# Two stacked blocks on one core: bias tables and a third gate unit earlier in the state-space loop, first units by input quarters, GpSimd's sum behind the level loop

## The chip, the cores and the metric

The kernel runs on one NeuronCore of a Trainium2 chip. Its time is the device time of one launch in microseconds (us), the median of three runs. TensorE (PE) multiplies, VectorE (DVE), ScalarE (ACT) and GpSimd (POOL) do the elementwise work, SyncE (SP) starts the loads of the weights. Every engine takes its own instructions in order; between engines there are only semaphores.

## The reference, cut to what matters

256 tokens of width 1024 pass through two blocks. All numbers are float32.

```python
# first block, two layers
h = rms_norm(x) * (1 + sc1) + sh1
x = x + gt1 * hybrid_mixer(h)           # w_in, gated delta rule, stick-breaking attention, w_out
h = rms_norm(x) * (1 + sc2) + sh2
x = x + gt2 * (swiglu(h) if l == 0 else moe_swiglu(h))   # d_ff 3584; top 2 of 8 experts
# second block, two layers
h = h + 0.5 * swiglu(rmsnorm(h))        # ffn1, d_ff 2816
u = rmsnorm(h)
h = h + (s5_mixer(u) if layer == 0 else nsa_mixer(u, kv))
h = h + 0.5 * swiglu(rmsnorm(h))        # ffn2
```

In the delta rule each of 16 chains (8 heads, 2 chunks) needs `decay = exp(g_i - g_j)` for the triangle that is kept, once for the matrix that is inverted and once, transposed, for `qk = (q k^T) * decay`. The S5 mixer is a complex diagonal recurrence over 256 steps for 64 groups of 64 states, then a GELU, then `y * sigmoid(y @ w_glu)`. The attention of the last layer adds a bias by the distance between query and key, one number per head out of a small table `rel_bias`; for the compressed keys these are 15 columns for each of 16 heads and two tiles of tokens.

## The kernel before, in words

**Weights.** All large weights lie in DRAM as units of 128 x 2048 numbers (1 MB). SP loads them into a ring of six buffers in the order of use; a buffer is loaded again when TensorE has reported the unit before in it as done (`unit_done`). For most units ScalarE writes a rounded high part (`w_hi`, line 2484, into one of two places), VectorE the rest (`w_low`, line 1384, as are all its plain two-input operations), and TensorE sums three products: high by high, high by low part of the input, low part by high (`product`, lines 523 to 525). A unit has 16 tiles, so 48 matmuls of 256 columns. Some units (the gate units of S5, w_kv, w_q, w_o) are multiplied in plain float32 instead, at two PE instructions a matmul (lines 464 and 1099).

**The first unit of a stage.** The input is split as well, in four quarters of two 128-row tiles: ScalarE writes the high part of quarter c (semaphore `h_high`, lines 2567 and 2525), VectorE the low part (`h_low`, lines 1384 and 1415). `cols_split` goes over the two output tiles t and, within t, over the eight input tiles k, with all three products of a tile together; for t = 0 it waits for `h_low` of a quarter before the quarter's first product, and t = 1 needs no wait any more. `cols_raw` is the form for the stages whose input isn't scaled by its norm yet (`ffn2_0`, `ffn2_1`): both t over k = 0 to 5, then both t over k = 6, 7, with the same waits. Behind it stands the sum of the squares for the norm (line 474). Seven stages begin in one of these ways: `w_in0`, `ffn`, `w_in1`, `ffn1_0`, `ffn2_0`, `ffn1_1`, `ffn2_1`.

**The S5 loop.** For each of eight rounds k: TensorE multiplies the input (`pair_inputs`, line 1134, banks 0 to 3), VectorE rotates the sums, scans twice (lines 2239, 2240) and rotates back; TensorE forms the outputs of the round (`pair_outputs`, lines 1149 to 1157, bank 4), ScalarE the GELU (`s5_gelu`, line 2856). TensorE's order by hand is: outputs of round k-1, inputs of round k+1, for k < 5 the transposes of matrices (line 480, into bank 5, copied out by ScalarE, semaphore `bt`), for k = 5, 6, 7 ten small products each of the bias table (`bias_tables`, line 1111, 32 rows by 16 columns, also into bank 5), and one row of the gate product for units 0 and 1 (`glu_row`, line 1099, banks 6 and 7). Units 2 and 3 of the gate go to banks 0 and 1, which are free once VectorE has read the last inputs; their rows 0 to 3 stand at k = 7, the rest after the last outputs. ScalarE's round is: GELU of round k-2, the row of magnitudes for the scan (line 2871), the copies of bank 5 for k < 5, a diagonal (line 2882). After the loop VectorE turns bank 5 into the bias table, ScalarE takes four sigmoids (line 2889), VectorE updates x and `ffn2_0` begins.

**The delta mixer.** The 16 triangular matrices are inverted in six levels (`squares`, line 610, and VectorE, lines 1384, 1883, 1891); `level_f` counts VectorE's updates of the inverse, ten in all. Beside it GpSimd makes the second decay: clamp (line 2999), add of a mask kept in `inverse_rms` (line 3001, reports `u_arg`), later two products (3003, 3005, reports `q_decayed`). ScalarE's order is: copies of qk (2752), two silus, wait for `u_arg`, exp (2756), two sigmoids of the gates (2758), then the copies that TensorE's `corner(1)` waits for (`neg_b`, line 2760) and those for `corner_b` (2762). TensorE's order there is: turn(2, 0) (line 653), corner(0), corner(1) (line 610), three more turns, z(0), z(1), the products for v_new (line 701).

Of the kernel before, what the change touches and what calls it, by code (L numbers as in the profile page):

```python
# [22 lines left out]
P = 128  # L23
# [68 lines left out]
def program(nc, A):  # L92
    ctx = ExitStack()
    with ctx:
# [5 lines left out]
        def sem(name):  # L100
            if name not in sems:
# [5 lines left out]
                         attn_tensor=("bias_ps", "hid_ps", "hid_t_ps", "cmp_ps", "kv_sum", "kv_vt", "kc_sum", "gate_logits",  # L107
                                      "cmp_logits"),
                         attn_scalar=("hid", "kv_rs", "kc_rs", "gate_exp", "cmp_exp"))
# [170 lines left out]
        GLU_BANK = (6, 7, 0, 1)  # L280
# [166 lines left out]
        def _(pe):  # L447
# [79 lines left out]
            def cols_raw(n, dst, room, name):  # L527

                for k0, k1 in ((0, 6), (6, KT)):
                    for t in range(2):  # L530
                        for k in range(k0, k1):
                            if t == 0 and k % 2 == 0:
                                pe.wait_ge(*at("h_low", k // 2 + 1, INPUTS[name]))
                            c = (k * 2 + t) * P
                            mm = product(dst(t), parts(w_high(room, n) + c, P), ring_low[n % RING][:, c:c + P],
                                         parts(h_high(room) + k * TOK, TOK), parts(HB + k * TOK, TOK), k == 0 and t == 0,
                                         k == KT - 1, skip_group_check=True)
                mm.then_inc(sem("unit_done"), 1)

            def cols_split(n, dst, room, first=None, low=HB):  # L540

                for t in range(2):
# [413 lines left out]
            def ffn_split(name, blocks, base, room):  # L956
# [3 lines left out]
                def step(p, i=0):  # L960
# [8 lines left out]
                    if which < 2:  # L969
# [3 lines left out]
                        if p == 0 and name in UNSCALED:  # L973
                            cols_raw(n, lambda t: half(0, t), room, name)
# [116 lines left out]
            def glu_row(k, first):  # L1091

                pe.wait_ge(sem("y_gelu"), k + 1)
                for u in (first, first + 1):
# [9 lines left out]
            def bias_tables(part):  # L1104

                if part == 0:
                    pe.wait_ge(sem("bt"), 6)
                for j in range(10 * part, 10 * part + 10):
                    n, c = divmod(j, NCMP)
                    x = 255 + n * P - 16 * c - 31  # L1110
                    mm = pe.matmul(bank[5][:, j * QH:(j + 1) * QH], con("onehot", P, x, pn=32),
                                   par("rel_bias", 16, pn=32), start=True, stop=True)

# [59 lines left out]
            pair_inputs(1)  # L1173
            for k in range(1, KT + 1):
# [8 lines left out]
                if k > 4 and k < KT:  # L1183
                    bias_tables(k - 5)
                if k > 1:
                    glu_row(k - 2, 0)
                if k == KT - 1:

                    pe.wait_ge(sem("bu_read"), KT)
                    for r in range(4):  # L1190
                        glu_row(r, 2)
            for r in range(4, KT - 1):
                glu_row(r, 2)
            glu_row(KT - 1, 0)
            glu_row(KT - 1, 2)
# [183 lines left out]
        def _(ve):  # L1379
# [872 lines left out]
            ve.wait_ge(*event("bias_ps"))  # L2252
            for n in range(NT):

                tt(view(BIG, CB + n * QH * NCMP, [[NCMP, QH], [1, NCMP]]), view(bank[5], n * QH * NCMP, [[1, QH], [QH, NCMP]]),
# [218 lines left out]
        def _(se):  # L2474
# [391 lines left out]
            for k in range(KT):  # L2866
# [15 lines left out]
                act(big(D_DIAG + k % 4 * P, P), ident, ACT.Copy, scale=par("s5_d", 1, k)).then_inc(sem("s5_scalar"), 1)  # L2882
            s5_gelu(KT - 2)
# [91 lines left out]
        def _(po):  # L2975
# [18 lines left out]
            for l in range(LAYERS):  # L2994
# [5 lines left out]
                b16 = view(BIG, SLOT["B"], [[P, 16], [1, P]])  # L3000
                po.tensor_tensor(b16, b16, view(RS, 0, [[0, 16], [1, P]]), ALU.add).then_inc(mixer("u_arg", l)[0], 1)
# [215 lines left out]
```

## Time and profile before

| | |
|---|---|
| median of three runs | 3108.93 us (3107.57 to 3109.07) |
| the profiled execution: its own time, its span | 3107.27 us, 3105.5 us |
| busy: PE, DVE, ACT, POOL | 97%, 73%, 52%, 2% |
| mean granted TensorE clock | 0.977 of 2.4 GHz |
| HBM read | 698.5 MB, 225 GB/s over the span |

The span runs from the first to the last instruction. In rows of the timeline the first number is the start in us from the start of the span, the second the duration; `xN` is how many instructions a row merges, and `[idle before <-releaser]` how long the engine had nothing to do before it and what ended that.

### The profile page before, as it was taken

How to read it: one execution, taken by the hardware profiler on the slowest of the kernel's cores; microseconds unless marked ns; L12 is line 12 of the kernel's file. 1: busy time of each engine (PE TensorE's matmuls, PEld its weight loads, DVE VectorE, ACT ScalarE, POOL GpSimd, SP SyncE). 2: the span in 40 equal slices, each digit the busy share in tenths (PEclk: the TensorE clock that was granted, in tenths of full speed). 3: DMA queues.
4: the chain of work that ended last, by engine and by line, in shares of the span. 5: the costliest groups of instructions: out<-in, count | busy, mean ns of one | idle time of the engine just before them, and what ended most of it. 6: DMA issues, size and time to landing. Idle time of an engine off the chain costs nothing.

```text
span 3105.5 us, 51419 instructions
## 1 busy us (share of the span) xinstructions
PE 3013.7 (97%) x21686; PEld 2740.2 (88%) x21686; DVE 2268.9 (73%) x2596; ACT 1624.5 (52%) x1604; POOL 74.2 (2%) x83
## 2 busy tenths in 40 slices
PE   7999999999999999999999999999899999998999
PEld 7998899999988788888888888899779999996899
DVE  7977688848685888888888888688665536547355
ACT  3444543435553777777777777543324414436333
POOL 0002000000010000000000000000000000000000
PEclk8999999989999999999999999999899999999999
DMA  8650488735403799999999999745234544540353
GB/s 358 253 190 2 159 312 314 259 113 183 150 2 136 256 365 370 366 366 367 371 364 365 370 366 367 268 164 187 97 123 176 181 158 150 202 163 28 125 187 122
DMA packets 130030, 703.14 MB, mean 226 GB/s; under 512 B 11184, under 2 KB 15552, under 8 KB 74048
## 3 DMA queue, kind: packets, MB, share of 16 engines
q1 hardware_dynamic: 118816, 650.30, 57.1%
q0 software_dynamic: 6880, 48.24, 4.0%
q8 instruction: 128, 2.10, 0.3%
q10 hardware_dynamic: 4160, 2.12, 0.3%
q14 instruction: 46, 0.38, 0.0%
HBM read 698.50 MB, written 1.07 MB: 225 GB/s over the span
## 4 chain that ended last, share of the span: by engine, by line
PE 91%; DVE 6%; ACT 2%; issue 1%; DMA 0%; SPq 0%; ACTq 0%; DVEq 0%
PE banks L523 25%; PE banks L524 25%; PE banks L525 25%; PE banks L464 3%; PE banks L474 1%; DVE ring_low L1384 1%; DVE tail L1384 1%; PE banks L610 1%; PE banks L1099 1%; DVE big L1384 1%; PE banks L851 1%; PE banks L519 1%; PE banks L872 1%; ACT parts L2484 0%; PE banks L1157 0%
## 5 line engine op out<-in xcount | busy, mean ns | idle before, releaser
L1384 DVE TENSOR_TENSOR ring_low<-ring,parts 128x2048 fp32r<-128x2048 f32 x586 | 1333.2, 2288 | 365.2 <-ACT parts L2484 339.6
L523 PE MATMUL banks<-parts 128*128 128x256 f32 (+1 forms) x3968 | 1240.1, 313 | 15.1 <-DVE tail_parts L1384 7.0
L524 PE MATMUL banks<-tail_parts,parts 128*128 128x256 f32 x3744 | 1060.5, 283 | 0.0
L2484 ACT ACTIVATE parts<-ring 128x2048 fp32r<-128x2048 f32 x250 | 479.1, 1917 | 776.3 <-PE banks L525 730.4
L525 PE MATMUL banks<-parts,ring_low 128*128 128x256 f32 x3072 | 868.7, 283 | 0.0
L523 PEld LDWEIGHTS banks<-parts 128*128 128x128 f32 x3968 | 753.7, 190 | 57.3 <-issue 12.4
L2586 ACT ACTIVATE parts<-ring 128x2048 fp32r<-128x2048 f32 x336 | 644.5, 1919 | 188.5 <-DMA ring<-in_wall 181.3
L524 PEld LDWEIGHTS banks<-tail_parts,parts 128*128 128x128 f32 x3744 | 710.9, 190 | 2.0 <-issue 1.9
L525 PEld LDWEIGHTS banks<-parts,ring_low 128*128 128x128 f32 x3072 | 584.5, 190 | 0.0
L525 PE MATMUL banks<-parts,tail_parts 128*128 128x512 f32 x896 | 352.6, 393 | 0.0
L524 PE MATMUL banks<-ring_low,parts 128*128 128x512 f32 x896 | 352.5, 393 | 0.0
L523 PE MATMUL banks<-tail_parts,parts 128*128 128x256 f32 x928 | 262.7, 283 | 0.1
L525 PE MATMUL banks<-tail_parts,ring_low 128*128 128x256 f32 x928 | 262.2, 283 | 0.0
L525 PEld LDWEIGHTS banks<-parts,tail_parts 128*128 128x128 f32 x896 | 168.3, 188 | 40.5
L524 PEld LDWEIGHTS banks<-ring_low,parts 128*128 128x128 f32 x896 | 168.8, 188 | 33.9
L523 PE MATMUL banks<-parts,tail_parts 128*128 128x512 f32 x448 | 177.5, 396 | 1.1 <-DVE tail_parts L1384 1.0
L523 PEld LDWEIGHTS banks<-tail_parts,parts 128*128 128x128 f32 x928 | 176.7, 190 | 0.4 <-issue 0.4
L525 PEld LDWEIGHTS banks<-tail_parts,ring_low 128*128 128x128 f32 x928 | 176.4, 190 | 0.0
L524 PE MATMUL banks<-ring_low,tail_parts 128*128 128x512 f32 x448 | 176.3, 394 | 0.0
L525 PE MATMUL banks<-parts 128*128 128x512 f32 x448 | 176.2, 393 | 0.0
L1384 DVE TENSOR_TENSOR tail_parts<-banks,tail_parts 128x256 fp32r<-128x256 f32 x112 | 47.4, 424 | 85.8 <-ACT tail_parts L2612 85.5
L1384 DVE TENSOR_TENSOR tail<-tail,banks 128x256 f32<-128x256 f32 (+1 forms) x164 | 81.7, 498 | 31.0 <-PE banks L525 19.4
(451 smaller groups left out, 3155.0 us busy)
## 6 DMA issues: line engine op xcount, KB each, us to landing
ring<-in_wall SPq DMA_DIRECT2D x616, 1024.0 KB, 6.1
big<-in_wall POOLq DMA_DIRECT2D x40, 1024.0 KB, 5.8
big<-in_w_k POOLq DMA_DIRECT2D x1, 2048.0 KB, 8.1
big<-in_w_v POOLq DMA_DIRECT2D x1, 2048.0 KB, 13.7
big<-bias_table ACTq DMA_DIRECT2D x2, 1024.0 KB, 7.2
constants<-in_con SPq DMA_DIRECT2D x1, 1249.5 KB, 9.3
x<-in_x SPq DMA_DIRECT2D x1, 1024.0 KB, 6.6
big<-big POOLq DMA_DIRECT2D x16, 64.0 KB, 5.1
```

The lines of the kernel that those rows point to most:

```text
L464: mm = pe.matmul(dst(t), tile(n, k * tiles + t), src[:, src_off + k * width:src_off + (k + 1) * width], start=(k == 0), stop=(k == kt - 1))
L474: mm = pe.matmul(half(b, 0), ones, big(SQ0 + t * TOK, TOK), start=(t == 0), stop=(t == KT - 1))
L519: mm = pe.matmul(o[:, c:c + 1], ada_sum(first + n)[:, t * P:(t + 1) * P], ones[:, 0:1], start=True, stop=True)
L523: pe.matmul(o, high, in_high, start=start, stop=False, **kw)
L524: pe.matmul(o, high, in_low, start=False, stop=False, **kw)
L525: return pe.matmul(o, low, in_high, start=False, stop=stop, **kw)
L610: mm = pe.matmul(bank[b][SQ * h:SQ * h + SQ, c % 8 * SQ:(c % 8 + 1) * SQ], lhs(c, h), rhs(c, h), start=True, stop=True)
L851: mm = pe.transpose(bank[6 + b % 2][:, f * P:(f + 1) * P], FG[:, b % 2 * 512 + f * P:b % 2 * 512 + (f + 1) * P], ident)
L872: mm = pe.matmul(bank[k][:, :], parts(source + n * 1024 + k * P, P), parts(SEL + n * 1024 + batch * 512, 512), start=(part == 0 and n == 0 ...
L1384: return ve.tensor_tensor(out, a, b, op)
L2484: act(parts(w_high(room, n), UNIT), ring[n % RING][:, :], ACT.Copy).then_inc(sem("w_high"), 1)
L2586: act(parts(slot_at(q), UNIT), ring[r][:, :], ACT.Copy).then_inc(sem("x_high"), 1)
```

## The change

It has three parts. None changes what is computed.

**1. The S5 loop.** The thirty bias products are made in two halves of fifteen, the first behind the inputs of round 1, the second at k = 1 behind the transposes, into bank 7. ScalarE copies them at k = 1 to `LNB` and `RS` (two new copies of 128 x 240), after a wait for the new event `bias_rows` and ahead of its GELU of round 0; TensorE waits for `bias_raw` at k = 2, before the gate product writes bank 7. Unit 2 of the gate moves to bank 5 and joins at k = 5, with its rows 0 to 2 first; unit 3 moves to bank 0.

**2. First units.** `cols_chunks` takes the place of `cols_raw` and of `cols_split` for a stage's first unit, where the low part lies at `HB`: for each quarter it waits for `h_high`, makes the eight products that need only the high part, waits for `h_low` and makes the other four.

**3. The delta mixer.** GpSimd's add waits for the tenth `level_f`.

```diff
-        GLU_BANK = (6, 7, 0, 1)
+        GLU_BANK = (6, 7, 5, 0)
...
+            def cols_chunks(n, dst, room, name):
+
+                for c in range(4):
+                    pe.wait_ge(*at("h_high", c + 1, INPUTS[name]))
                     for t in range(2):
-                        for k in range(k0, k1):
...
+                        for k in (2 * c, 2 * c + 1):
+                            w = (k * 2 + t) * P
+                            high = parts(h_high(room) + k * TOK, TOK)
+                            pe.matmul(dst(t), parts(w_high(room, n) + w, P), high, start=(k == 0 and t == 0), stop=False,
+                                      skip_group_check=True)
+                            pe.matmul(dst(t), ring_low[n % RING][:, w:w + P], high, start=False, stop=False, skip_group_check=True)
+                    pe.wait_ge(*at("h_low", c + 1, INPUTS[name]))
+                    for t in range(2):
+                        for k in (2 * c, 2 * c + 1):
+                            mm = pe.matmul(dst(t), parts(w_high(room, n) + (k * 2 + t) * P, P), parts(HB + k * TOK, TOK), start=False,
+                                           stop=(k == KT - 1), skip_group_check=True)
                 mm.then_inc(sem("unit_done"), 1)
 
             def cols_split(n, dst, room, first=None, low=HB):
 
+                if first is not None and low == HB:
+                    cols_chunks(n, dst, room, first)
+                    return
...
             pair_inputs(1)
+            bias_table(0)
             for k in range(1, KT + 1):
                 pair_outputs(k - 1)
...
                     turn_matrices(k + 3, bank[5]).then_inc(sem("bt_ps"), 1)
-                if k > 4 and k < KT:
-                    bias_tables(k - 5)
+                if k == 1:
+                    bias_table(1).then_inc(event("bias_rows")[0], 1)
+                if k == 2:
+                    pe.wait_ge(*event("bias_raw"))
+                if k == 5:
+                    pe.wait_ge(sem("bt"), 6)
+                    for r in range(k - 2):
+                        glu_row(r, (2,))
                 if k > 1:
-                    glu_row(k - 2, 0)
+                    glu_row(k - 2, (0, 1) if k < 5 else (0, 1, 2))
                 if k == KT - 1:
 
                     pe.wait_ge(sem("bu_read"), KT)
                     for r in range(4):
-                        glu_row(r, 2)
+                        glu_row(r, (3,))
             for r in range(4, KT - 1):
-                glu_row(r, 2)
-            glu_row(KT - 1, 0)
-            glu_row(KT - 1, 2)
+                glu_row(r, (3,))
+            glu_row(KT - 1, (0, 1, 2, 3))
...
                 act(big(D_DIAG + k % 4 * P, P), ident, ACT.Copy, scale=par("s5_d", 1, k)).then_inc(sem("s5_scalar"), 1)
+                if k == 1:
+                    se.wait_ge(*at("normed", KT, 6))
+                    se.wait_ge(*event("bias_rows"))
+                    act(LNB[:, 0:QH * NCMP], bank[7][:, 0:QH * NCMP], ACT.Copy)
+                    act(RS[:, 0:QH * NCMP], bank[7][:, QH * NCMP:2 * QH * NCMP], ACT.Copy).then_inc(event("bias_raw")[0], 1)
...
                 b16 = view(BIG, SLOT["B"], [[P, 16], [1, P]])
+                po.wait_ge(*at("level_f", 2, l, 2 * LEVELS - 2))
                 po.tensor_tensor(b16, b16, view(RS, 0, [[0, 16], [1, P]]), ALU.add).then_inc(mixer("u_arg", l)[0], 1)
```

## Rows read from the trace of the kernel before

**Rows 1.** The page, its chain that ended last, by engine.

```profile
PE 91%; DVE 6%; ACT 2%; issue 1%; DMA 0%; SPq 0%; ACTq 0%; DVEq 0%
```

**Rows 2.** Timeline of DVE in the S5 loop: start, us, engine, operation, idle before.

```profile
2219.26 1.22 DVE L1384 TENSOR_TENSOR big<-banks,big 128x1024 f32<-128x1024 f32 x1
...
2240.87 1.22 DVE L2239 TENSOR_TENSOR_SCAN big<-small,big 128x512 f32<-128x512 f32 x1 [1.20 <-ACT small L2871]
...
2245.59 1.22 DVE L1384 TENSOR_TENSOR tail<-big 128x1024 f32<-128x1024 f32 x1 [1.12 <-PE banks L1157]
...
2287.86 1.22 DVE L1384 TENSOR_TENSOR tail<-big 128x1024 f32<-128x1024 f32 x1
```

**Rows 3.** Timeline of PE at the loop's head, outputs of rounds 0 and 1.

```profile
2227.76 1.22 PE L1149 MATMUL banks<-tail,big 128*128 128x256 f32 x2 [4.59 <-DVE tail L1384]
...
2240.34 1.19 PE L1149 MATMUL banks<-tail,big 128*128 128x256 f32 x2 [3.85 <-ACT big L2856]
```

**Rows 4.** Timeline of PE at the loop's end.

```profile
2285.51 2.40 PE L1111 MATMUL banks<-parameters,constants 32*128 32x16 f32 x20
2287.84 8.90 PE L1099 MATMUL banks<-big,ring 128*128 128x256 f32 x40
...
2299.96 10.63 PE L1099 MATMUL banks<-big,ring 128*128 128x256 f32 x48
```

**Rows 5.** Timelines of DVE, ACT and PE at the start of ffn2_0.

```profile
2317.49 0.88 DVE L1415 SCALAR_TENSOR_TENSOR tail_parts<-x,parameters,parts 128x256 fp32r<-128x256 f32 x2 [0.25 <-ACT parts L2525]
...
2320.50 2.19 ACT L2531 ACTIVATE tail<-x 128x512 f32<-128x512 f32 x4
...
2323.56 3.62 PE L474 MATMUL banks<-tail,constants 128*128 128x256 f32 x16
```

**Rows 6.** Timeline of PE in the first units of ffn, ffn1_0 and ffn1_1.

```profile
386.51 0.55 PE L523 MATMUL banks<-parts 128*128 128x256 f32 x1 [3.95 <-DVE tail_parts L1384]
...
390.81 0.39 PE L523 MATMUL banks<-parts 128*128 128x256 f32 x1 [0.37 <-DVE tail_parts L1384]
...
2021.23 0.39 PE L523 MATMUL banks<-parts 128*128 128x256 f32 x1 [0.41 <-DVE tail_parts L1384]
...
2577.10 0.36 PE L523 MATMUL banks<-parts 128*128 128x256 f32 x1 [1.88 <-DVE tail_parts L1384]
```

**Rows 7.** Timelines of POOL and DVE in the delta mixers of layers 0 and 1.

```profile
245.15 4.52 POOL L3001 TENSOR_TENSOR big<-big,inverse_rms 128x2048 f32<-128x2048 f32 x1
...
246.55 3.67 DVE L1384 TENSOR_TENSOR tail<-constants,big 128x512 f32<-128x512 f32 x1
251.58 0.69 DVE L1384 TENSOR_TENSOR tail<-constants,big 128x512 f32<-128x512 f32 x1
...
271.15 0.65 DVE L1384 TENSOR_TENSOR tail<-tail,banks 128x512 f32<-128x512 f32 x1
...
853.57 4.56 DVE L1384 TENSOR_TENSOR tail<-constants,big 128x512 f32<-128x512 f32 x1
```

**Rows 8.** Windows: us, busy PE, PEld, DVE, ACT, POOL, granted clock, DMA, GB/s.

```profile
252.00:256.00 4.00, 3.92 (x74) 3.74 (x72) 2.25 (x4) 3.97 (x3) 2.43 (x1) 0.50 0.01 4
...
2328.00:2332.00 4.00, 4.00 (x36) 4.00 (x35) 2.02 (x1) 3.23 (x3) 0.00 (x0) 1.00 0.02 4
```

**Rows 9.** Timeline of ACT in the first mixer, from the exp on.

```profile
251.59 1.91 ACT L2756 ACTIVATE big<-big 128x2048 f32<-128x2048 f32 x1
253.51 1.28 ACT L2758 ACT_TABLE_LOAD   x1
254.81 3.71 ACT L2758 ACTIVATE big<-big 128x2048 f32<-128x2048 f32 x2
278.84 0.59 ACT L2760 ACTIVATE tail<-banks 64x512 f32<-64x512 f32 x1 [20.32 <-PE banks L638]
```

**Rows 10.** Timeline of PE in the first mixer, both corners, three turns.

```profile
279.76 2.08 PE L610 MATMUL banks<-tail,big 64*64 64x64 f32 x32
281.76 2.84 PE L653 MATMUL banks<-constants,big 128*128 128x128 f32 x24
```

More of the change, by code:

```diff
@@ L106, in program @@
                                       "k_normed", "cmp_arg", "cmp_p"),
-                         attn_tensor=("bias_ps", "hid_ps", "hid_t_ps", "cmp_ps", "kv_sum", "kv_vt", "kc_sum", "gate_logits",
+                         attn_tensor=("bias_rows", "bias_ps", "hid_ps", "hid_t_ps", "cmp_ps", "kv_sum", "kv_vt", "kc_sum", "gate_logits",
                                       "cmp_logits"),
-                         attn_scalar=("hid", "kv_rs", "kc_rs", "gate_exp", "cmp_exp"))
+                         attn_scalar=("bias_raw", "hid", "kv_rs", "kc_rs", "gate_exp", "cmp_exp"))
         def event(name):
@@ L525, in product @@
                 return pe.matmul(o, low, in_high, start=False, stop=stop, **kw)
-            def cols_raw(n, dst, room, name):
-                for k0, k1 in ((0, 6), (6, KT)):
+            def cols_chunks(n, dst, room, name):
+                for c in range(4):
+                    pe.wait_ge(*at("h_high", c + 1, INPUTS[name]))
                     for t in range(2):
-                        for k in range(k0, k1):
[L532 to L537, printed above, removed]
+                        for k in (2 * c, 2 * c + 1):
[9 more added lines that the diff above has]
+                                           stop=(k == KT - 1), skip_group_check=True)
                 mm.then_inc(sem("unit_done"), 1)
             def cols_split(n, dst, room, first=None, low=HB):
+                if first is not None and low == HB:
+                    cols_chunks(n, dst, room, first)
+                    return
                 for t in range(2):
@@ L973, in step @@
                         if p == 0 and name in UNSCALED:
-                            cols_raw(n, lambda t: half(0, t), room, name)
+                            cols_chunks(n, lambda t: half(0, t), room, name)
                             norm(7 if name == "ffn2_0" else 11, NORM_BANK[7 if name == "ffn2_0" else 11], RAW_SQ)
@@ L1089, in _, with glu_row @@
             pe.wait_ge(sem("bt"), 1)
-            def glu_row(k, first):
+            def glu_row(k, units):
                 pe.wait_ge(sem("y_gelu"), k + 1)
-                for u in (first, first + 1):
+                for u in units:
                     n = UN["glu"] + u
@@ L1102, in glu_row, with bias_table @@
                         mm.then_inc(sem("unit_done"), 1)
[L1104 to L1109, printed above, removed]
+            def bias_table(n):
+                for c in range(NCMP):
                     x = 255 + n * P - 16 * c - 31
-                    mm = pe.matmul(bank[5][:, j * QH:(j + 1) * QH], con("onehot", P, x, pn=32),
+                    j = n * NCMP + c
+                    mm = pe.matmul(bank[7][:, j * QH:(j + 1) * QH], con("onehot", P, x, pn=32),
                                    par("rel_bias", 16, pn=32), start=True, stop=True)
+                return mm
             def distance_table():
@@ L2252, in _ @@
             ve.wait_ge(*event("bias_ps"))
+            ve.wait_ge(*event("bias_raw"))
             for n in range(NT):
-                tt(view(BIG, CB + n * QH * NCMP, [[NCMP, QH], [1, NCMP]]), view(bank[5], n * QH * NCMP, [[1, QH], [QH, NCMP]]),
+                tt(view(BIG, CB + n * QH * NCMP, [[NCMP, QH], [1, NCMP]]), view((LNB, RS)[n], 0, [[1, QH], [QH, NCMP]]),
                    view(CON, CC["cmp_add"] + n * NCMP, [[0, QH], [1, NCMP]]), ALU.add)
```

## The prediction

> **What bounds the kernel now.** I read the page's chain first: 91% of the chain that ended last is TensorE [rows 1]. In the long stages its products follow one another without a gap, and nothing in this change touches them. So I went on to the waits, looking for the stretches where TensorE waits or runs at half its clock, and then to the timelines of the three places that the change edits. The reader is to see three things. In the S5 loop VectorE works nearly without a break from 2219.26 to 2289.1 us [rows 2], and TensorE waits for it in the first rounds [rows 3] but is behind it in the last: the outputs of the last round could start at 2289.1, and start after 2296.7, where a backlog of gate products ends [rows 4]. In the first unit of a stage TensorE waits for VectorE's low parts [rows 6]. In the delta mixer one VectorE addition that takes 0.69 us alone takes 3.67 and 4.56 us [rows 7]. Everything else between is rigid: a microsecond won in one of these places should arrive at the end, since the loads follow TensorE's reports through a ring of six.
>
> The sum is made against the profiled execution's own time, 3107.27 us; the median of the runs shown is 3108.93, that is 1.7 more, and I carry the difference over unchanged.
>
> **Part 1, the S5 loop: the end of it.** A PE instruction of the gate product costs 8.90 / 40 = 0.22 us, a table product (two instructions) 2.40 / 10 = 0.24 [rows 4]. From 2285.5 on TensorE has today: ten table products 2.3, 40 gate instructions 8.9, the distance table and the outputs together about 3.3 (2296.7 to 2300.0), 48 gate instructions 10.6, end 2310.6 [rows 4]. After the change the rounds 5 and 6 hold 24 and 12 gate instructions in place of 20 table and 8 gate instructions each: 5.3 and 2.6 us for 4.0 and 4.0. So round 5 is a microsecond longer, inside a wait for VectorE, and round 6 ends before VectorE has its result, so the outputs of round 6 start about 1.2 us earlier than today and run into no backlog. Then: outputs 2280.7 to 2283.4, 12 + 16 gate instructions 6.1 us to 2289.5, just at VectorE's 2289.1; distance table and outputs 3.3 to 2292.8; 12 + 12 + 16 = 40 instructions 8.8 us to 2301.5. That is 9.1 us before today's 2310.6. What is late next is nothing: the GELU of the last round and the split of the first `ffn2_0` unit move with the outputs and stay ahead of the last row.
>
> **Part 1, the head of it.** The first fifteen table products fall into a gap of 4.59 us [rows 3]. At full clock they cost 15 x 0.24 = 3.6 us and are hidden; at half clock, which this gap has, up to 7.2, and the outputs of round 0 start 2.6 us late. The trace before has no such products at half clock, so I keep both ends and take the middle, 1.2 us late at the transposes of k = 1. The second fifteen fall into the gap of 3.85 us before 2240.34 [rows 3], 3.6 us at full clock. But now ScalarE is queued behind them: its two copies (new; nearest are its GELUs of 128 x 256 from a bank, 0.3 to 0.4 each) come ahead of its table switch of 1.28 [rows 9] and its GELU, and behind that stands the row of magnitudes that VectorE's scan waited for already, 1.20 us at 2240.87 [rows 2]. Chain: transposes end 2236.5 + 1.2, table products to 2241.2, copies to 2241.9, table and GELU to 2243.5, magnitudes to 2243.9. VectorE's scan starts 3.1 us late. It gets back the 1.12 us that it waits today for the outputs of round 1 [rows 2], if these run at full clock after a shorter idle time, and some of the next wait. I take the loop's head at +1.6 us, between +0.4 (all at full clock) and +4.2 (both halves at half clock). It shifts the end one for one: part 1 is -9.1 + 1.6 = -7.5 us, between -8.7 and -4.9. The new waits of TensorE (`bias_raw` at k = 2, `bt` at k = 5) are met long before.
>
> **Part 2, first units.** A unit is 48 products; 36 took 4.00 us at full clock, 0.11 to 0.12 each [rows 8], and twice that at 1.2 GHz. Where TensorE arrives last, nothing is won: `w_in0` and `w_in1` stand behind the beta gates, and `ffn2_1` starts when the low part of its weights is there and never waits again. These three are 0. The other four:
> - `ffn`: it started at 386.51 after 3.95 us of waiting and waited 0.37 us again at 390.81 [rows 6]. The high part of a quarter is there about 0.7 us before its low part (one VectorE operation of 0.69, the length of the one at 251.58 [rows 7]). -0.7 -0.4, and 30 products stand after the last quarter today, 12 then, so the half-clock stretch costs less: -1.4.
> - `ffn1_0`: two waits inside the unit, 0.4 each (one shown) [rows 6], and the drain before each: -1.3. The low weights of unit 1 end 0.1 us before the new end, so no more than this.
> - `ffn1_1`: it started at 2577.10 after 1.88 us [rows 6]: -0.7 for the start, -0.6 inside. The low weights of unit 1 are ready 2 us before today's end of the unit, which caps this at -2.0. I take -1.3.
> - `ffn2_0`: the last quarter's low part is ready at 2318.37, but today 36 products stand behind the third quarter and the norm's sum begins at 2323.56 [rows 5]. In quarters the unit ends at 2319 to 2321. Then the sum meets a new wait: ScalarE's squares start at 2320.50 and end at 2322.7 [rows 5], so the sum can't end before 2323.6, and in order takes 3.6 us from 2321.1: 2324.7 instead of 2327.2. -2.3, between -3.5 and 0 (the sum at half clock).
>
> The first of these gains shifts all that follows, so they add: -6.3 us, between -9 and -2.
>
> **Part 3, the delta mixer.** GpSimd's add ran from 245.15 to 249.67, and VectorE's addition with both inputs in SBUF, started at 246.55, ended at 250.22; the same operation at 251.58 took 0.69 [rows 7]. Out of the way this gives 2.98 us in layer 0 and 3.87 in layer 1. The idle TensorE fell to 1.2 GHz behind it [rows 8], which made the next level about 1.1 us longer: -4.1 and -5.0.
>
> At its new place the add starts behind the tenth update, 271.15 + 0.65 = 271.8 in today's time, and ends at 276.4. VectorE's operations beside it there have an input in a bank, and such operations ran undisturbed beside GpSimd's products today. But ScalarE waits in order. After `u_arg` it has the exp, 1.91, a switch of tables, 1.30, and two sigmoids, 3.71 [rows 9], so it is free at 276.45 + 6.92 = 283.4. The copy for `neg_b`, today at 278.84 to 279.43 [rows 9], ends at 284.0. TensorE's corner(1), which is the second half of the row at 279.76 and so begins at 280.8 [rows 10], waits until 284.05: +3.25 us, and behind it in the queue stand the three turns, z(0), z(1) and the products for v_new, for which VectorE has nothing to do instead. This is a critical stretch: the turns alone are 2.84 us [rows 10]. And TensorE, idle for 3.25 us, may fall to 1.2 GHz as it did at 252 [rows 8]. That row is 4 us wholly at half clock, which would cost 2.0 of its work; with the edges of such a dip I take 2.3, between 0 (the clock stays up) and 3.4 (VectorE's own share of the turns hides the rest). So layer 0 is 3.25 + 2.3 - 4.1 = +1.4, layer 1 is 3.25 + 2.3 - 5.0 = +0.6: part 3 is +2.0 us, between -2.6 (clock kept in both) and +4.2. GpSimd's later products end 285.4, before VectorE asks for them.
>
> The Trainium skill (ScalarE: Activation LUTs, What ACT_TABLE_LOAD costs) puts a switch of tables at about 2.66 us with its drain; here the row after the load at 253.51 starts 1.30 us later [rows 9], so I see no drain on the path. By the page each of the two delays at `neg_b` and the one at the first GELU would be 1.4 us longer, and the sum -7.6 instead of -11.8.
>
> **Sum.** -7.5 - 6.3 + 2.0 = -11.8 us: 3107.3 - 11.8 = 3095.5 by the profiled execution, 3097.1 by the median. Forecast 3097.
>
> **Rivals.**
> 1. *The mixer gains in full*: ScalarE's late copy costs little, because TensorE keeps its clock over the wait and the chain behind has slack. For it: the wait is short. Against it: the turns are followed at once by work that VectorE needs. If corner(1) cost nothing, part 3 would be -9.1 and the time 3097.1 - 11.1 = 3086; with the wait but no clock loss 3092. I give 3089 for it.
> 2. *The loop's head eats the tail, and the quarters give little*: both halves of the table products at half clock, +4.2 and TensorE's part at half clock after it, and first units that only stretch over the same half-clock time, -2.5 in all; the mixer at +4.2. Part 1 -4.9: sum -3.2, time 3106, within the measurement of before. For it: both gaps at the head are at half clock today.
> 3. *Slower, by the clock*: the quarters leave TensorE waiting eight times in a first unit instead of four, and it stays at 1.2 GHz through that unit and beyond in each of the five edited FFN stages. The price is 0.11 us for each product at half clock that is at full clock today; it decides from 11.8 / 0.11 = 107 such products, two more units and a bit. Four units would make -11.8 + 21 = +9, time 3118. Against it: every dip seen ends while a unit goes on.
> 4. *The quarters do nothing*, because the low weights of unit 1 or ScalarE's squares end last everywhere: part 2 is 0, time 3103.
>
> **How the numbers follow.** A measurement of this kernel can tell 0.2% from no change, that is 6.2 us: faster is below 3102.7, slower above 3115.1. Chances: the forecast 0.62, rival 1 0.13, rival 2 0.14, rival 3 0.04, rival 4 0.07. The forecast's own range, from its bounds taken together, is 3091 to 3103. The range for 8 in 10 is 3088 to 3104: it takes in rival 1 at its likely size and rival 4, and leaves out rivals 2 and 3. Faster: 0.62 + 0.13, and 0.02 of rival 4, 0.77; slower 0.04; the rest, 0.19, within.
>
> **What would show it.** Part 1: the first gate row ends and the sigmoids start 7 to 8 us earlier against the loop's start, the outputs of the last round no longer behind a backlog; VectorE's scan of round 2 some 3 us later than today and a loop of about 71.4 us instead of 69.8. Part 2: PE rows of 8 and 4 products by turns, the sum for `ffn2_0` beginning as soon as a square is there. Part 3: the VectorE addition at 0.69 us, the copy for `neg_b` right behind the sigmoids, TensorE idle about 3.2 us before corner(1), its clock at 0.5 behind that. The prediction is wrong if TensorE doesn't wait at corner(1), if the head of the loop is late by more than 4 us, or if a first unit ends no earlier than today against the end of its norm.

## The result, and the profile after

The changed kernel takes 3084.11 us (median of 4 runs, 3082.07 to 3087.08) against 3108.25 us before: ratio 0.9924, interval 0.9913 to 0.9936. It is faster by 24.1 us, twice the 11.8 us that were forecast, and it ends below the range. The profiled execution took 3083.18 us, its span is 3081.4 us.

The error is one term, and it is a reading error. The line `po.wait_ge(*at("level_f", 2, l, ...))` waits for the second of the ten updates in a layer, not for the tenth: in `at(name, count, stage, total)` the 2 is the count. The title, the description of the change above and the prediction put the add behind the tenth update, at the end of the level loop, and are wrong there. GpSimd's add stands right behind the two VectorE additions that it used to block, not at the end of the level loop.

By the page of the changed kernel the engines are busy for 97% (TensorE), 73% (VectorE), 53% (ScalarE) and 2% (GpSimd) of the span: in shares next to nothing has moved. The waits show the change. What TensorE waited for, before (engine, line, releaser: us in total, times, longest):

```profile
PE banks L610 <- DVE tail L1384: 9.2, 8, 4.5
PE banks L523 <- DVE tail_parts L1384: 8.0, 6, 4.0
PE banks L523 <- DVE tail_parts L1415: 4.1, 3, 2.6
PE banks L1149 <- DVE tail L1384: 7.0, 3, 4.6
PE banks L1149 <- ACT big L2856: 3.8, 1, 3.8
```

The same view after (L610 is now L618, L1384 is L1397, L1149 is L1156, and the first products of a unit are L535):

```profile
PE banks L618 <- DVE tail L1397: 4.5, 12, 0.9
PE banks L535 <- ACT parts L2581: 4.4, 2, 3.2
PE banks L1156 <- DVE tail L1397: 3.3, 3, 2.1
PE banks L1156 <- issue: 2.5, 1, 2.5
...
PE banks L535 <- ACT parts L2539: 1.6, 1, 1.6
```

**Where the time came from.** I cut both traces at rows that both have: the start of the first products of the delta mixer (L603, after L611), of the output product behind it (L464 x32) and of each norm's sum (L474 x16). From the chain of waits, before and then after:

```profile
237.49 7.14 PE banks L603 x64
315.81 6.91 PE banks L464 x32
...
844.50 7.14 PE banks L603 x64
923.71 6.91 PE banks L464 x32
...
2211.56 3.47 PE banks L474 x16
2323.72 3.45 PE banks L474 x16
```

```profile
236.99 7.14 PE banks L611 x64
311.13 6.91 PE banks L464 x32
...
840.02 7.14 PE banks L611 x64
914.16 6.91 PE banks L464 x32
...
2199.26 3.47 PE banks L474 x16
2302.36 3.72 PE banks L474 x16
```

| stretch | before | after | difference | forecast |
|---|---|---|---|---|
| mixer of layer 0 | 78.32 | 74.14 | -4.18 | +1.4 |
| mixer of layer 1 | 79.21 | 74.14 | -5.07 | +0.6 |
| S5: loop start to the gate's end | 91.3 | 84.8 | -6.5 | -7.5 |
| `ffn`: norm's sum to first unit's end | 15.5 | 14.1 | -1.4 | -1.4 |
| `ffn1_0`: final norm's first product (L1074) to first unit's end | 17.9 | 16.3 | -1.6 | -1.3 |
| `ffn2_0`: gate's end to norm's sum | 13.0 | 10.6 | -2.4 | -2.3 |
| `ffn1_1`: norm's sum to the next one | 259.5 | 257.7 | -1.8 | -1.3 |

They add up to -23.0, and the two profiled executions differ by 24.1. The last microsecond is the sum of larger differences in stretches that nothing edits, among them these: the rest of the `ffn` stage is 1.6 us longer than before, and the stretch behind `ffn1_0`'s first unit, the attention stretch and the start of the kernel are 1.2, 1.2 and 0.5 us shorter.

The column "before" is one execution, and two of its rows are not the same in the other kernels that have the old code there. Layer 1's mixer takes 78.1 and 78.4 us in the second and third experiments, where VectorE's addition is as long as before (4.57 and 4.56 us); it takes 74.1 in every kernel with the wait for the second update. `ffn`'s first unit in the old order ends 15.5 us after the norm's sum began here, 15.6, 16.3 and 17.0 in the fifth, second and first experiments, and 14.1 in every kernel that has `cols_chunks` as in the change. In the first experiment, with the 17.0, the unit starts at 383.2 and the granted clock is 0.50 from 384 to 390 us; in the kernel before it starts at 386.5, and the clock is 0.55 and 0.60 up to 390 and 1.00 from there. So layer 1's gain is 4.0 to 5.1 us and `ffn`'s 1.4 to 2.8, by how long TensorE stays at the lower clock behind the wait.

**The mixer.** GpSimd, VectorE and ScalarE of layer 0 after, as answers to [rows 7, 9]:

```profile
248.94 4.54 POOL L3021 TENSOR_TENSOR big<-big,inverse_rms 128x2048 f32<-128x2048 f32 x1 [4.00 <-DVE tail L1397]
```

```profile
246.05 0.69 DVE L1397 TENSOR_TENSOR tail<-constants,big 128x512 f32<-128x512 f32 x1
...
248.10 0.69 DVE L1397 TENSOR_TENSOR tail<-constants,big 128x512 f32<-128x512 f32 x1
```

```profile
253.51 1.91 ACT L2770 ACTIVATE big<-big 128x2048 f32<-128x2048 f32 x1 [2.44 <-POOL big L3021]
...
256.74 3.71 ACT L2772 ACTIVATE big<-big 128x2048 f32<-128x2048 f32 x2
274.15 0.59 ACT L2774 ACTIVATE tail<-banks 64x512 f32<-64x512 f32 x1 [13.71 <-PE banks L646]
```

Both additions take 0.69 us, the add starts 0.15 us after the second ends, and ScalarE, done at 260.45, stands idle for 13.71 us before the copy for `neg_b`. So corner(1) waits for nothing. The same window is at full clock now, and so is the one right behind the additions (248.80 to 252.80); it was at 0.50 [rows 8]:

```profile
252.00:256.00 4.00, 3.65 (x116) 3.38 (x112) 3.30 (x7) 2.47 (x2) 1.98 (x2) 1.00 0.02 4
```

**The head of the loop.** PE, then ACT, then DVE after, as answers to [rows 2, 3]:

```profile
2210.43 5.51 PE L1117 MATMUL banks<-parameters,constants 32*128 32x16 f32 x30
2215.87 1.22 PE L1156 MATMUL banks<-tail,big 128*128 128x256 f32 x2
...
2224.84 3.52 PE L1117 MATMUL banks<-parameters,constants 32*128 32x16 f32 x30
2230.89 1.19 PE L1156 MATMUL banks<-tail,big 128*128 128x256 f32 x2 [2.53 <-issue]
```

```profile
2228.45 0.37 ACT L2900 ACTIVATE log_mean_square<-banks 128x240 f32<-128x240 f32 x1 [1.50 <-PE banks L1117]
...
2229.10 1.28 ACT L2870 ACT_TABLE_LOAD   x1
```

```profile
2206.96 1.21 DVE L1397 TENSOR_TENSOR big<-banks,big 128x1024 f32<-128x1024 f32 x1
...
2231.42 1.22 DVE L2252 TENSOR_TENSOR_SCAN big<-small,big 128x512 f32<-128x512 f32 x1 [4.06 <-ACT small L2885]
...
2235.84 1.23 DVE L1397 TENSOR_TENSOR tail<-big 128x1024 f32<-128x1024 f32 x1 [0.82 <-PE banks L1164]
...
2277.66 1.22 DVE L1397 TENSOR_TENSOR tail<-big 128x1024 f32<-128x1024 f32 x1
```

Thirty narrow instructions take 3.5 us at full clock. The first thirty take 5.5, since the granted clock falls from 1.00 to 0.50 about a microsecond after they begin (0.92 in the window 2211.00 to 2211.50, 0.50 in all that follow up to 2216). The scan waits for 4.06 us in place of 1.20. Counted from the loop's first row (2219.26 before, 2206.96 after) it starts 2.85 us later than before, the row at 2235.84 2.55 later, and VectorE's last row in the loop, 2287.86 before and 2277.66 after, 2.1 later. That last number is the head's cost in this execution.

**The end of the loop and `ffn2_0`**, PE after, as answers to [rows 4, 5]:

```profile
2273.32 6.31 PE L1107 MATMUL banks<-big,ring 128*128 128x256 f32 x28
...
2282.85 8.90 PE L1107 MATMUL banks<-big,ring 128*128 128x256 f32 x40
2293.32 0.36 PE L535 MATMUL banks<-parts 128*128 128x256 f32 x1 [1.57 <-ACT parts L2539]
...
2302.36 3.72 PE L474 MATMUL banks<-tail,constants 128*128 128x256 f32 x16 [1.74 <-ACT tail L2545]
```

The 28 and the 40 instructions are those of the forecast, at its prices (6.1 and 8.8). The sum waits 1.74 us for ScalarE's squares, as forecast.

### The profile page after: what moved, and what is told of

It is laid out like the page before. It is cut to its first block, busy times and chain, and to the rows that moved or that the text cites. A ratio compares the mean times of both kernels' runs of the same rounds, so it can differ in the third digit from the quotient of the medians.

```text
span 3081.4 us, 51425 instructions
## 1 busy us (share of the span) xinstructions
PE 3001.8 (97%) x21686; PEld 2730.1 (89%) x21686; DVE 2264.2 (73%) x2596; ACT 1623.6 (53%) x1606; POOL 74.3 (2%) x83
## 4 chain that ended last, share of the span: by engine, by line
PE 90%; DVE 6%; ACT 2%; issue 1%; DMA 1%; SPq 0%; ACTq 0%; DVEq 0%
PE banks L523 24%; PE banks L524 24%; PE banks L525 24%; PE banks L464 3%; PE banks L474 1%; DVE ring_low L1397 1%; DVE big L1397 1%; DVE tail L1397 1%; PE banks L519 1%; PE banks L859 1%; PE banks L618 1%; PE banks L535 1%; PE banks L541 1%; PE banks L537 1%; DMA ring<-in_wall 1%
## 5 line engine op out<-in xcount | busy, mean ns | idle before, releaser
L1397 DVE TENSOR_TENSOR ring_low<-ring,parts 128x2048 fp32r<-128x2048 f32 x586 | 1335.4, 2288 | 363.6 <-ACT parts L2498 331.7
L523 PE MATMUL banks<-parts 128*128 128x256 f32 (+1 forms) x3792 | 1184.9, 312 | 3.8 <-ACT big L2665 2.2
L524 PE MATMUL banks<-tail_parts,parts 128*128 128x256 f32 x3568 | 1007.5, 282 | 0.0
L525 PE MATMUL banks<-parts,ring_low 128*128 128x256 f32 x2896 | 815.9, 282 | 0.0
L523 PEld LDWEIGHTS banks<-parts 128*128 128x128 f32 x3792 | 716.6, 189 | 42.9 <-issue 2.6
L524 PEld LDWEIGHTS banks<-tail_parts,parts 128*128 128x128 f32 x3568 | 673.6, 189 | 2.0 <-issue 1.9
L525 PEld LDWEIGHTS banks<-parts,ring_low 128*128 128x128 f32 x2896 | 547.6, 189 | 0.0
L523 PE MATMUL banks<-tail_parts,parts 128*128 128x256 f32 x928 | 262.7, 283 | 0.2 <-DVE ring_low L1397 0.2
L523 PEld LDWEIGHTS banks<-tail_parts,parts 128*128 128x128 f32 x928 | 176.8, 190 | 0.4 <-issue 0.4
L1397 DVE TENSOR_TENSOR tail_parts<-banks,tail_parts 128x256 fp32r<-128x256 f32 x112 | 47.5, 424 | 79.9 <-ACT tail_parts L2626 79.3
L1397 DVE TENSOR_TENSOR tail<-tail,banks 128x256 f32<-128x256 f32 (+1 forms) x164 | 81.8, 498 | 30.9 <-PE banks L525 20.2
```

What stands on the lines that cost most here:

```text
L523: pe.matmul(o, high, in_high, start=start, stop=False, **kw)
L524: pe.matmul(o, high, in_low, start=False, stop=False, **kw)
L525: return pe.matmul(o, low, in_high, start=False, stop=stop, **kw)
L1397: return ve.tensor_tensor(out, a, b, op)
```

## The experiments

All ratios are against the kernel before. Line numbers are those of the kernel named.

**1 to 3. Each part alone.** The first kernel is before with this line only:

```diff
                 b16 = view(BIG, SLOT["B"], [[P, 16], [1, P]])
+                po.wait_ge(*at("level_f", 2, l, 2 * LEVELS - 2))
```

> The kernel before with GpSimd's wait alone (part 3). Theory A: the wait is for the second level_f, so the add starts when VectorE's second addition with both inputs in SBUF is done, nothing is delayed by it, and the whole stall goes: 2.98 + 3.87 us of VectorE and some 1.1 + 1.1 us of TensorE's half clock behind it, -9.1 us against before (between -8 and -10.5); VectorE's addition at 0.69 us in both layers. Rival B: most of the 24 us came from the other two parts, and this one is worth under 4 us.

Measured: 3099.45 us, ratio 0.9970 (0.9960 to 0.9980), 8.5 us faster, where 9.1 were expected. The mixers take 74.13 and 74.14 us, the same as after.

The second is before with the edits of the S5 loop only (`bias_table`, `glu_row`, `GLU_BANK`, the two copies):

> The kernel before with the change in the S5 loop alone (part 1). From the two traces: gate product ends 6.6 us earlier against the loop's start (8.6 won at the end, 2.0 lost at the head), so -6.6 us (-5 to -8.5). Rival B: the gain of this part is larger, 9 us or more, because the head costs nothing when the gaps before it are as before.

Measured: 3098.70 us, ratio 0.9970 (0.9959 to 0.9982), 9.3 us faster. From the loop's norm to the next it takes 106.2 us instead of 112.2, 6.0 less: 5.1 up to the gate's end and 0.9 behind it. Another 3.9 are in the attention stretch, 142.4 us instead of 146.3, where no line differs. The loop itself has the edits of the changed kernel and gains 5.1 us where that one gains 6.5. The rows show why, PE and then DVE:

```profile
2223.08 6.41 PE L1109 MATMUL banks<-parameters,constants 32*128 32x16 f32 x30
```

```profile
2244.78 1.23 DVE L2244 TENSOR_TENSOR_SCAN big<-small,big 128x512 f32<-128x512 f32 x1 [5.19 <-ACT small L2877]
```

Here the clock is down when the first narrow instructions begin (0.55 from 2222 to 2224, then 0.50), and they take 6.4 us. The scan waits 5.19 us instead of 4.06, and VectorE's last row in the loop comes 3.6 us later than before, counted from the loop's first row, not 2.1. From that row to the gate's end it is 14.1 us in both kernels, against 22.7 with the old loop. So the end's gain is the same, and the head's cost is not: it goes by when the clock falls.

The third is before with `cols_chunks` only:

> The kernel before with the first units by quarters alone (part 2). From the two traces: ffn -1.4, ffn1_0 -1.2, ffn2_0 -2.3, ffn1_1 -1.8, the others nothing: -6.7 us (-5 to -8). Rival B: the quarters are worth 10 us or more, since the later stages gain as well.

Measured: 3099.01 us, ratio 0.9972 (0.9961 to 0.9983), 8.9 us faster. The split stages gain the same as in the changed kernel (`ffn` -1.4, `ffn1_0` -1.6, `ffn2_0` -2.4, `ffn1_1` -1.8), 7.2 together, where 6.7 were expected; the rest of the 8.9 us is in stretches that no line of this part touches. The three parts alone add up to 26.7 us, together they give 24.1: within their intervals, 3 us to either side for each, they add.

**4. The add where I had put it.** The changed kernel with the wait that I had read into it:

```diff
-                po.wait_ge(*at("level_f", 2, l, 2 * LEVELS - 2))
+                po.wait_ge(*at("level_f", 2 * LEVELS - 2, l, 2 * LEVELS - 2))
```

> The changed kernel with GpSimd's wait at the tenth level_f, not the second: the place that the prediction priced. Theory A (the pricing was right, the place was wrong): the copy for neg_b comes right behind the two sigmoids, TensorE waits 3.25 us at corner(1) in each layer and loses 0 to 3.4 us more by its clock, so it is 6.5 to 13.3 us slower than the changed kernel, about 3095 us, 11 to 13 us faster than before. Rival B (the pricing was wrong too): TensorE doesn't wait there, and the time is that of the changed kernel, 3084 us.

Measured: 3095.78 us, ratio 0.9964 (0.9950 to 0.9977), 11.7 us slower than the changed kernel. The profiled execution was the fastest of five, 3091.29 us, 8.1 more than that of the changed kernel. The mixers take 79.02 and 79.09 us, 4.9 more each. ACT, PE and the window behind:

```profile
272.05 1.91 ACT L2770 ACTIVATE big<-big 128x2048 f32<-128x2048 f32 x1 [20.75 <-POOL big L3021]
...
275.27 3.71 ACT L2772 ACTIVATE big<-big 128x2048 f32<-128x2048 f32 x2
278.88 0.57 ACT L2774 ACTIVATE tail<-banks 64x512 f32<-64x512 f32 x1
```

```profile
279.56 1.64 PE L618 MATMUL banks<-tail,big 64*64 64x64 f32 x16 [3.12 <-issue]
281.13 3.89 PE L661 MATMUL banks<-constants,big 128*128 128x128 f32 x24
```

```profile
280.00:284.00 4.00, 4.00 (x29) 3.88 (x28) 1.55 (x3) 1.88 (x2) 0.99 (x1) 0.58 0.00 0
```

This is the chain of the prediction's third part, row for row: the copy right behind the sigmoids, 3.12 us of idle TensorE before corner(1) (forecast 3.25), then the turns at 3.89 us in place of 2.84 at a granted clock of 0.58. The profile names "issue" and not ScalarE as the releaser, but corner(1) starts 0.1 us after the copy at 278.88 ends. The price is 4.9 us a layer, where I had 5.55. So the mechanism and its price hold; it belongs to another kernel than the one that was to be predicted. The five runs of this kernel lie between 3091.3 and 3098.9 us, so that their median comes so near to 3097 is in part luck.

**5. What blocks VectorE.** Before, with GpSimd's add in two halves at its old place:

```diff
-                po.tensor_tensor(b16, b16, view(RS, 0, [[0, 16], [1, P]]), ALU.add).then_inc(mixer("u_arg", l)[0], 1)
+                b8 = [view(BIG, SLOT["B"] + x * 1024, [[P, 8], [1, P]]) for x in range(2)]
+                po.tensor_tensor(b8[0], b8[0], view(RS, 0, [[0, 8], [1, P]]), ALU.add)
+                po.tensor_tensor(b8[1], b8[1], view(RS, 0, [[0, 8], [1, P]]), ALU.add).then_inc(mixer("u_arg", l)[0], 1)
```

> The kernel before, with GpSimd's add made as two adds of half the size (2.26 us each) at its old place. Theory A (VectorE's addition with both inputs in SBUF is held until the GpSimd instruction that runs is over, and gets its turn between two): in layer 0 it ends near 248.1 in today's time, some 1.5 us long instead of 3.67, in layer 1 some 2.4 us instead of 4.56; the second such addition may meet the second half and be held up to 1 us. 2 to 4 us faster than before. Rival B (it is held for as long as GpSimd has work of this kind): 3.67 and 4.56 as before, time as before.

Measured: 3107.84 us, ratio interval 0.9986 to 1.0005, no difference in time where 2 to 4 us were expected, but the rows are clear. GpSimd, then VectorE, layer 0:

```profile
246.08 2.36 POOL L3002 TENSOR_TENSOR big<-big,inverse_rms 128x1024 f32<-128x1024 f32 x1
248.40 2.81 POOL L3003 TENSOR_TENSOR big<-big,inverse_rms 128x1024 f32<-128x1024 f32 x1
```

```profile
247.58 1.41 DVE L1384 TENSOR_TENSOR tail<-constants,big 128x512 f32<-128x512 f32 x1
...
250.34 1.42 DVE L1384 TENSOR_TENSOR tail<-constants,big 128x512 f32<-128x512 f32 x1
```

One addition of 3.67 us and one of 0.69 [rows 7] have become two of 1.4. The first gets in when the first half ends at 248.44, and the second half takes 2.81 us instead of 2.36, as if it had waited for the addition in its turn. The mixers gain 1.2 and 1.6 us of the 4.2 and 5.1 that the new place gives, 2.8 in all, too little for this measurement; against the other executions of the old layer 1, at 78.1 and 78.4 us, the second is 0.5 to 0.8. The Trainium skill (SBUF — State Buffer, SBUF: two separate sides) says that VectorE with two inputs in SBUF and a GpSimd operation that reads SBUF exclude each other for a whole instruction. The rows agree.

**6 and 7. The head of the loop.** The changed kernel with ScalarE's two copies a round later, behind the GELU and the row of magnitudes:

```diff
+                if k == 2:
+                    se.wait_ge(*at("normed", KT, 6))
+                    se.wait_ge(*event("bias_rows"))
+                    act(LNB[:, 0:QH * NCMP], bank[7][:, 0:QH * NCMP], ACT.Copy)
...
-                if k == 1:
-                    se.wait_ge(*at("normed", KT, 6))
-                    se.wait_ge(*event("bias_rows"))
-                    act(LNB[:, 0:QH * NCMP], bank[7][:, 0:QH * NCMP], ACT.Copy)
...
```

> The changed kernel, with ScalarE's two copies of the bias products moved behind the GELU of round 0 and the magnitudes of round 2. Theory A (the loop's head is late because the GELU and the magnitudes stand behind the wait for bias_rows): VectorE's wait before the scan of round 2 falls from 4.06 to about 2 us, the outputs of round 1 start some 2 us earlier, the loop is about 1.5 to 2 us shorter. Rival B (TensorE's fifteen products themselves are what delays the head): the wait falls by under 0.5 us.

Measured: 3083.26 us, ratio 0.9915 (0.9902 to 0.9929), 0.9 less than the changed kernel, not to be told from it. VectorE's scan waits 1.94 us instead of 4.06, and the next norm's sum comes 2.35 us earlier against the one before the loop. But that sum then takes 5.41 us instead of 3.72:

```profile
2302.14 5.41 PE L474 MATMUL banks<-tail,constants 128*128 128x256 f32 x16 [1.73 <-ACT tail L2545]
```

```profile
2302.00:2306.00 4.00, 3.86 (x10) 3.12 (x11) 0.47 (x1) 1.65 (x4) 0.00 (x0) 0.57 1.01 426
```

The work and the wait ahead of it are those of the changed kernel (1.73 against 1.74 us), the granted clock isn't: 0.57 in this window. That gives 1.7 of the 2.35 us back in this execution.

The seventh takes the sixth and loads the GELU's table ahead of its wait:

```diff
+                if k == 1:
+                    se.preload_act_table_set("gelu_apprx_tanh_and_others")
```

> As the kernel with the later copies, and the table of the GELU loaded at the start of ScalarE's round 1, where it waits for VectorE anyway. Theory A: another 1.28 us less before the GELU of round 0, so VectorE's wait before the scan of round 2 is under 1 us; TensorE's outputs of round 1 then start when its fifteen products end, about 2228.4 in the time of the changed kernel instead of 2230.9. Together 2 to 3 us faster than the changed kernel, 3081 to 3082 us. Rival B: VectorE waits for TensorE's outputs of round 1 instead, and the loop gains 1 us or less.

Measured: 3084.10 us, ratio 0.9922 (0.9909 to 0.9936). Rival B is what the rows show: the scan waits no more, and VectorE waits at the next row for TensorE's outputs instead:

```profile
2235.71 1.23 DVE L1397 TENSOR_TENSOR tail<-big 128x1024 f32<-128x1024 f32 x1 [2.01 <-PE banks L1164]
```

From norm to norm it is 100.5 us, 0.25 less than the sixth. So the copies made the scan 2.1 us later, and under them TensorE is the next to be late. With the copies out of the way the head costs nothing: from VectorE's first row in the loop to its last it is 68.0 and 68.1 us in these two kernels, 70.7 in the changed one and 68.6 before. Neither gain shows in the time. In the seventh the sum takes 3.72 us again, but the stretch from the second layer's norm to the S5 norm takes 1224.1 us instead of 1221.8 and the attention stretch 146.7 instead of 145.1, and no line differs in either: a gain of 2.5 us in the loop is below what these runs can tell by the total.

**8. The backlog.** The changed kernel with unit 2 of the gate back at the end, beside unit 3:

```diff
-                if k == 5:
-                    pe.wait_ge(sem("bt"), 6)
-                    for r in range(k - 2):
-                        glu_row(r, (2,))
...
-                    glu_row(k - 2, (0, 1) if k < 5 else (0, 1, 2))
+                    glu_row(k - 2, (0, 1))
...
+                    pe.wait_ge(sem("bt"), 6)     # at k = 7, before rows 0 to 3
...
-                glu_row(r, (3,))
+                glu_row(r, (2, 3))
```

> The changed kernel, but gate unit 2 is multiplied with unit 3 at and behind the last round again (still in bank 5). Theory A (what the loop's end won is work moved off TensorE: 20 gate instructions of 0.22 us, 4.4 us, and ten table products, 2.3, with 1.2 and more from round 6): the gate product ends 4 to 5 us later against the loop's start than in the changed kernel, 3088 to 3089 us. Rival B (the tables were all of it): no later by more than 1 us.

Measured: 3091.86 us, ratio 0.9945 (0.9930 to 0.9960), 7.7 us slower than the changed kernel; the stretch from norm to norm is 5.9 us longer. The backlog of before is there again, PE at the loop's end:

```profile
2277.40 8.90 PE L1107 MATMUL banks<-big,ring 128*128 128x256 f32 x40
...
2289.51 10.63 PE L1107 MATMUL banks<-big,ring 128*128 128x256 f32 x48
```

Not all of the 5.9 us are its doing. The head, which this edit doesn't touch, is 1.6 us later than in the changed kernel, with the first narrow products at 6.41 us as in the second experiment. From VectorE's last row to the gate's end it is 22.7 us before, 14.1 in the changed kernel and 18.4 here: 4.3 more, where 4 to 5 were expected. So of the 8.6 us that the end of the loop gained, half is the gate unit inside it, and half is there without it, from the table products that left rounds 5 to 7. Whether the unit would have found room with the tables still there was not run.

**9. Earlier start or even spread.** The changed kernel, each quarter waiting for both parts:

```diff
-                    pe.wait_ge(*at("h_high", c + 1, INPUTS[name]))
+                    pe.wait_ge(*at("h_low", c + 1, INPUTS[name]))
```

> The changed kernel, but each quarter of a first gate unit waits for both groups of the normalised input (level h_low, the later one) before its first product, as the first unit of before does; the order of the 16 products by quarters stays. So the split stages keep the even spreading over four quarters and lose only the earlier start. Theory A (what the quarters give is the earlier start on the first group): each split stage loses most of its gain; in the four stages with a gap of that kind (ffn, ffn1_0, ffn2_0, ffn1_1) about 1.4, 1.3, 2.3 and 1.3 us at most, so the time comes near 3088 to 3091 us against the changed kernel's 3084. Theory B (it is the quarters' order that pays, because a quarter's activation starts while the next quarter's products run): the stages lose 0.3 to 0.7 us each, together 1 to 3 us, and the time stays at 3084 to 3087 us; the wait ahead of the first product of the unit is longer by about 0.5 us in either case.

Measured: 3083.68 us, ratio 0.9931 (0.9909 to 0.9952), the same as the changed kernel. By stages the gains are -0.7, -1.4, -2.4 and -1.8 us, where the changed kernel has -1.4, -1.6, -2.4 and -1.8. The earlier start is worth 0.7 us in `ffn` and 0.2 in `ffn1_0`. It is worth nothing in `ffn2_0`, where ScalarE's squares end last in both kernels, and nothing in `ffn1_1`, where the second unit waits for the low part of its own weights (0.48 us after, none here). Theory B: 6.3 of the 7.2 us are the order by quarters, in `ffn` by the execution in the table; against the longer ones there the order gives more, and the start the same 0.7.

## Why the prediction was wrong, point by point

- **What bounds the kernel**: right. 23.0 of the 24.1 us are in the three places named. That each microsecond arrives at the end is borne out within a few microseconds and no closer, since other stretches move by that much.
- **Part 3, the saving** (-4.1 and -5.0): right, -4.18 and -5.07, the clock's share included. In layer 1 that share, 1.1 us, is that of the one execution the forecast was made from; against the old layer 1 in the second and third experiments the saving is 4.0 and 4.2.
- **Part 3, the cost. This is the step that failed**: "the add starts behind the tenth update, 271.15 + 0.65". It starts behind the second, at 248.94. All that followed, the late `u_arg`, ScalarE's queue of 6.9 us and corner(1) waiting 3.25 us plus 2.3 of clock, 11.1 us for two layers, does not happen in this kernel. With the cost at nothing the prediction's own terms give -7.5 - 6.3 - 9.1 = -22.9 us and a time of 3086, inside the measured runs. The fourth experiment has the wait where I read it, and there the time is 3095.8 against a forecast of 3097.
- **Part 1, the end** (-9.1): -8.6, in the second experiment too. The counts of gate instructions and their price hold, and the outputs of the last round meet no backlog.
- **Part 1, the head** (+1.6): +2.1, and +3.6 and +3.7 in the second and eighth experiments, whose head is the same; all are inside the bounds of +0.4 and +4.2. Forecast and measured lateness of the scan are 3.1 and 2.85 us, by the chain that was named (table products, copies, table, GELU, magnitudes). The first half, for which I gave 0 to 2.6 us, made the outputs of round 0 only 0.4 us later, mostly at the lower clock, and 1.7 in the second experiment. VectorE got back less than hoped, because TensorE stood idle for 2.53 us and fell to the lower clock again (0.50 from 2231 to 2234). When the clock falls was the unknown between the bounds: in this kernel a microsecond into the first table products, in the second experiment before they begin.
- **Part 2** (-6.3): -7.2. Each stage is within 0.5 us. The cap in `ffn2_0` (ScalarE's squares) was right. The reason was half right: I had priced the start at 0.7 us in `ffn` and `ffn1_1`, and the ninth experiment shows that in the second of these the start gives nothing and the quarters' order all. That `ffn` came out at the forecast -1.4 is in part luck, since the old order took up to 1.4 us longer there in other kernels.
- **Rivals**: the first (the mixer gains in full) is what the time looks like, but for a reason I had not written down. Had I checked which event the wait counts, it would have been the forecast. The second and the fourth are refuted by the tail's and the stages' rows, though the head alone came near the second's price for it (3.6 and 3.7 us of 4.2) in two experiments; the third by the mean granted clock, 0.982 against 0.977 before. The Trainium skill's larger price for a table switch with its drain (ScalarE: Activation LUTs, What ACT_TABLE_LOAD costs) is not seen here either: the load at 2229.10 is followed by the GELU at 2230.39, 1.29 us later.
- **Range**: it was made from the unknown costs of a mechanism. No bound in it stood for having read the code wrong, and the error, 12.3 us of change, was as large as the forecast. The bounds of the three terms all added up give 3089 to 3106, which leaves 3084 out as well.

**What stays open.** Stretches with the same code differ between kernels by up to 4 us: the attention stretch takes 142.4 to 146.7 us, the `ffn` stage from norm to norm 258.3 to 262.2 in the kernels with its old first unit and 256.9 to 260.1 in those of the changed one, and the stretch from the second layer's norm to the S5 norm, with `ffn1_0` in it, 1223.2 to 1227.4 and 1220.8 to 1224.1. The places followed to a row (`ffn`'s first unit, the head of the loop, the sum in the sixth experiment) differ by the granted clock; whether the others are the same, and what decides where it falls, was not settled.

## What to carry to other kernels

Before a wait is priced, read the definition of the helper that makes it and write down which event it counts and the time of that event in the trace; the price of its consequences comes after. A long GpSimd operation that reads SBUF costs a VectorE operation with two SBUF inputs the rest of its length, so place it by what VectorE does beside it, and ask what is queued behind its result. When the first unit of a stage waits for its input piece by piece, order the products by pieces: it gained even where nothing started earlier. And before a small gain behind an idle TensorE is booked, look at the same stretch in other kernels with the same code: the clock's share of it is not the same in each.

## What the runs showed of the hardware

- The same sum of squares, after the same wait, took 3.72 us in one kernel and 5.41 in another, at a granted clock of 1.00 and of 0.57: in that execution 1.7 of the 2.35 us saved just ahead of it were lost again. By its total, a change of 1 or 2 us can't be told from such differences in this kernel.
- GpSimd's add in two halves let VectorE in between: 1.41 and 1.42 us in place of 3.67 and 0.69.
- Thirty fp32 instructions of 32 rows by 16 columns took 3.52 us at full clock and 6.41 where the granted clock was 0.50 nearly throughout (second experiment), 1.8 times as long. In the changed kernel they took 5.51 us, the clock falling a microsecond after they began.
